# Sixteen row buffers, one block, and one stream of expert rows on VectorE

## The chip, the cores and the metric

The kernel runs on one core of a Trainium2 chip. The metric is the device time of one execution in microseconds, the median of several runs. The work below is done by the core's five engines (TensorE for matrix products, VectorE and ScalarE for elementwise work, GpSimd, which here only issues gathers, and SyncE, which issues the plain DMA transfers) and its 16 DMA engines.

## The reference, cut to what matters

Two networks run one after the other over 256 tokens of width 1024. The first has two layers; each ends in a PEER block. Per token it picks 128 experts of 16384 (8 heads, 16 each), takes a dot product of the token with each expert's row of `peer_u`, and adds up rows of `peer_v` weighted by gate and GELU:

```python
def expert_block(args):
    hb, ib, gb = args
    u = peer_u[ib]
    act = jax.nn.gelu(jnp.einsum('btd,bthkd->bthk', hb, u), approximate=False)
    return jnp.einsum('bthk,bthkd->btd', gb * act, peer_v[ib])
```

The second network has a context branch `z` that doesn't depend on the first network: a feed-forward block, a short convolution, a feed-forward block (its layer 0), then a feed-forward block and the attention's context keys and values (its layer 1):

```python
z = ffn_sublayer(z, mz, 0, g[0], g[1], ffn_w_gu[i, 0], ffn_w_down[i, 0])
hz = adaln_in(z, g[2], mz[3], mz[4])
yz = short_conv_mixer(hz, conv_w_in[j], conv_w[j], conv_w_out[j])
z = adaln_out(z, yz, g[3], mz[5], 1.0)
z = ffn_sublayer(z, mz, 6, g[4], g[5], ffn_w_gu[i, 1], ffn_w_down[i, 1])
```

## The kernel before

The expert phase stands twice in the kernel, once for each layer of the first network. The expert rows are gathered and used beside the context branch of the second network, which needs TensorE and the weights' DMA.

One expert row here means one gather: for each of the 128 tokens of a tile (one per partition) one row of 1024 floats, 512 KB in all. A layer has 512 of them: 256 of `peer_u` (128 for each of two token tiles; called feature rows below) and then 256 of `peer_v` (value rows). `Experts.fetch` (line 1728) issues them from GpSimd, each into the next of `GR = 8` buffers of the arena, after waiting until the row that used the buffer is done (`row_used`). `Experts.use` (line 1763) works on VectorE by heads of 16 rows. A feature row is a multiply and sum with the token's features, which stand in PSUM (line 1792, a custom instruction and a read of its accumulator); its result goes to one of 16 cells, which line 1797 copies out after each head. A value row is a multiply and add into PSUM (line 1788); it waits for its own row (`row_landed`) and for the row before it (`row_used`); line 1777 copies 16 weights into the cells ahead of each head. `enter_tile` (line 1746) changes the token tile.

The context branch is a chain of stages, each a block of its own. At the end of a block all engines meet before any starts the next. In each stage VectorE has the stage's own work and a whole number of heads beside it, written out in the order in which they run:

- `context_norm` (829): ScalarE squares and scales, TensorE turns, ScalarE makes the features. 1 head of rows; the first two rows go ahead of the reciprocal.
- `gate_up` (1886): 11 tiles of 64 matmuls; ScalarE a SiLU (1913) and VectorE a product (1931) for each. 5 heads, 8 rows for each of ten tiles.
- `down` (2040): 8 tiles of 44 matmuls; ScalarE copies and squares. 3 heads.
- `context_add` (2152): a chain of six small and large steps on VectorE (2168 to 2175), then 1 head.
- `conv_projection` (2272): 6 tiles of 64 matmuls; 3 heads. VectorE takes the products of tiles 4 and 5 (2322). `conv_taps` (2329): VectorE alone, 25 instructions, then 1 head. `project_out` (2100): 2 tiles of 32 matmuls, 1 head. `context_keys` (2406): 64 matmuls, 1 head.
- `weigh` (1819): GELU on ScalarE and the product with the gates, both over all 256 cells of a partition. It stands between the feature rows and the value rows.
- `alone` (1802): the heads that are left, in a loop on VectorE, with no context work beside them.

Layer 0 runs ffn z00 (10 heads), conv (6 heads), `weigh`, the convolution's add (1 head), ffn z01 (10 heads), and 5 heads alone. Layer 1 runs ffn z10 (10 heads), norm and keys (2 heads), 4 heads alone, `weigh`, and 16 heads alone.

The weights come through `WeightStream` (line 148): SyncE loads half a tile at a time into `raw`, which holds two tiles. Context weights are used as they are. For other stages they are split into `w_hi` and `w_lo`; these two tensors, 4096 floats each per partition, are idle in the expert phase. The loads of a next stage's first two tiles are issued at the end of the stage before.

TensorE's, ScalarE's and VectorE's programs are written out instruction by instruction in most of these stages; loops stand in `gate_up` (pairs of tiles, on all three) and in `alone` (VectorE). GpSimd's gathers are all written out.

## Time and profile before

| | |
|---|---|
| median of 3 runs | 4243.65 us (4240.59 to 4245.16) |
| the profiled execution's own time | 4238.47 us |
| its span | 4236.7 us |
| expert phase of layer 0 (from its first norm to the last row) | 591.6 to 1567.9 us |
| expert phase of layer 1 | 2131.3 to 2955.5 us |
| busy, of the span: TensorE, VectorE, ScalarE, GpSimd | 64%, 63%, 23%, 23% |

The page cuts the span into 40 slices of about 106 us, a digit for each in tenths. Expert phases are where GpSimd (POOL) is busy:

```profile
PE   6776649937389308676569610000798698977698
DVE  3635686674777795544966778998645555545554
POOL 0000024452454540000044556665000000000000
DMA  6543679997799974432789999998344244541153
```

In the slices of the expert phases DMA stands at 7 to 9 tenths, and the last four of layer 1 have TensorE at 0: these are the rows without context work.

### The profile page before, as it was taken

The page shows a single profiled execution, that of the slowest core. Times are in us where ns is not written, and L with a number is a line of the kernel's source. Part 1 is how long each engine was busy: PE and PEld are TensorE (multiplying, and loading weights), DVE is VectorE, ACT ScalarE, POOL GpSimd, SP SyncE. Part 2 cuts the span into 40 slices and gives each one's busy share as a digit, 9 for nine tenths or more (in the row PEclk, how much of TensorE's full clock was granted, in tenths as well). Part 3 has the DMA queues.
Part 4 walks back from the last instruction along what each step waited for, and adds up shares of the span by engine and source line. Part 5 has one row for each costly group of instructions (what it writes and reads, how often), then busy time and mean ns, then how long its engine had stood idle before and what let it go on. Part 6 is the DMA issues. An engine that isn't in the chain of part 4 may idle for free. (4 is left out here: it accounts for less than half of the span.)

```text
span 4236.7 us, 44741 instructions
## 1 busy us (share of the span) xinstructions
PE 2721.9 (64%) x16804; PEld 2359.7 (56%) x16804; DVE 2673.1 (63%) x3884; ACT 982.5 (23%) x1358; POOL 961.8 (23%) x1028
## 2 busy tenths in 40 slices
PE   6776649937389308676569610000798698977698
PEld 5555428835178307475258610000798598975498
DVE  3635686674777795544966778998645555545554
ACT  2333210010110003332110000000444344533343
POOL 0000024452454540000044556665000000000000
PEclk8978769967699759787679855555899799988899
DMA  6543679997799974432789999998344244541153
GB/s 236 192 160 108 243 310 381 412 374 278 288 390 412 378 296 161 169 128 98 314 310 413 394 347 358 367 377 327 130 158 156 103 160 149 166 144 44 40 186 112
DMA packets 229372, 1034.40 MB, mean 244 GB/s; under 512 B 29657, under 2 KB 32617, under 8 KB 180073
## 3 DMA queue, kind: packets, MB, share of 16 engines
q0 software_dynamic: 147456, 536.94, 32.7%
q1 hardware_dynamic: 81768, 495.51, 32.3%
q8 instruction: 91, 1.49, 0.1%
q14 instruction: 57, 0.46, 0.0%
HBM read 1031.30 MB, written 1.05 MB: 244 GB/s over the span
## 5 line engine op out<-in xcount | busy, mean ns | idle before, releaser
L270 DVE TENSOR_TENSOR w_lo<-raw,w_hi 128x1024 fp32r<-128x1024 f32 (+1 forms) x492 | 558.6, 1138 | 700.2 <-ACT w_hi L257 699.7
L1740 POOL DMA_INDIRECT arena_layer<-in_peer_u,arena_layer x512 | 481.3, 940 | 1632.6 <-SPq L833 1165.8
L1788 DVE SCALAR_TENSOR_TENSOR ps<-arena_layer,ps 128x1024 f32<-128x1024 f32 x512 | 660.2, 1290 | 85.8 <-DMA arena_layer<-in_peer_v,arena_layer 50.8
L1792 DVE CUSTOM_DVE_ANT_0 arena_layer<-arena_layer,ps 128x1024 f32<-128x1024 f32 x512 | 608.8, 1219 | 147.4 <-DMA arena_layer<-in_peer_u,arena_layer 121.5
L628 PE MATMUL ps<-hT_hi,w_hi 128*128 128x256 f32 x2240 | 644.7, 288 | 70.7 <-PEq L763 31.6
L257 ACT ACTIVATE w_hi<-raw 128x1024 fp32r<-128x1024 f32 (+1 forms) x492 | 485.1, 989 | 796.3 <-PE ps L628 795.1
L628 PE MATMUL ps<-hT_lo,w_hi 128*128 128x256 f32 x2240 | 642.8, 287 | 0.0
L628 PE MATMUL ps<-hT_hi,w_lo 128*128 128x256 f32 x2240 | 642.2, 287 | 0.0
L628 PE MATMUL ps<-parts_context,raw 128*128 128x256 f32 x2496 | 568.3, 390 | 94.2 <-issue 78.6
L628 PEld LDWEIGHTS ps<-parts_context,raw 128*128 128x128 f32 x2496 | 487.4, 196 | 174.8 <-issue 106.6
L1740 POOL DMA_INDIRECT arena_layer<-in_peer_v,arena_layer x512 | 480.3, 938 | 351.5 <-DVE ps L1788 251.1
L628 PEld LDWEIGHTS ps<-hT_hi,w_hi 128*128 128x128 f32 x2240 | 437.9, 195 | 74.4 <-issue 74.4
L628 PEld LDWEIGHTS ps<-hT_lo,w_hi 128*128 128x128 f32 x2240 | 437.8, 195 | 0.0
L628 PEld LDWEIGHTS ps<-hT_hi,w_lo 128*128 128x128 f32 x2240 | 437.5, 195 | 0.0
L886 PE MATMUL ps<-ident,adacol 128*128 128x128 f32 x96 | 18.9, 378 | 650.2 <-PEq L1804 627.2
L886 PEld LDWEIGHTS ps<-ident,adacol 128*128 128x128 f32 x96 | 17.7, 284 | 651.1 <-issue 651.1
L628 PE MATMUL ps<-raw,parts_context 128*128 128x256 f32 (+1 forms) x1184 | 277.0, 397 | 24.4 <-issue 24.4
L628 PEld LDWEIGHTS ps<-raw,parts_context 128*128 128x128 f32 x1184 | 228.5, 193 | 71.5 <-issue 41.6
L628 PE MATMUL ps<-w_hi,parts_ffn_x 128*128 128x256 f32 x1408 | 257.8, 286 | 3.7 <-PEq L1891 3.7
L628 PEld LDWEIGHTS ps<-w_hi,parts_ffn_x 128*128 128x128 f32 x1408 | 223.0, 195 | 3.9 <-issue 3.9
L690 PE MATMUL ps<-raw,cond 128*32 128x512 f32 x960 | 171.2, 820 | 80.1 <-DMA raw<-in_w_mod 32.2
L628 PE MATMUL ps<-w_lo,parts_ffn_x 128*128 128x256 f32 x704 | 200.9, 285 | 0.0
(361 smaller groups left out, 2957.4 us busy)
## 6 DMA issues: line engine op xcount, KB each, us to landing
raw<-in_ffn_w_gu SPq DMA_DIRECT2D x154, 1024.0 KB
raw<-in_w_mod SPq DMA_DIRECT2D x72, 1024.0 KB
raw<-in_w_ada SPq DMA_DIRECT2D x48, 1024.0 KB
raw<-in_w_in SPq DMA_DIRECT2D x44, 1024.0 KB
raw<-in_ffn_w_down SPq DMA_DIRECT2D x56, 768.0 KB
raw<-in_ffn_w_down SPq DMA_DIRECT2D x56, 640.0 KB
raw<-in_conv_w_in SPq DMA_DIRECT2D x24, 1024.0 KB
raw<-in_w_o SPq DMA_DIRECT2D x8, 1024.0 KB
```

The lines of the kernel that those rows point to most:

```text
L257: act.activation(self.hi[:, k, 0:g.chunks[k] * g.cols], self.raw_part(g, parity, k // 2, g.starts(k), g.starts(k + 1)), ACT.Copy).then_inc ...
L270: dve.tensor_tensor(self.lo[:, k, 0:n], self.raw_part(g, parity, k // 2, g.starts(k), g.starts(k + 1)), self.hi[:, k, 0:n].bitcast(F32), A ...
L628: mm = pe.matmul(out_, stay, move, start=start and n == 0, stop=stop and n == len(combos) - 1, skip_group_check=True)
L690: mm = pe.matmul(ps[at:at + STRIP, unit, 0:512], cond[:, k, :], part[:, c, :], start=k < STRIPS, stop=k >= KC - STRIPS, skip_group_check=True)
L886: mm = pe.matmul(ps[:, unit, c * P:(c + 1) * P], column(c).to_broadcast([P, P]), ident[:], start=True, stop=True)
L1740: gp.indirect_dma_start(self.grow[:, slot % GR, :], None, self.tables[slot // half_way], bass.IndirectOffsetOnAxis(ap=self.index[:, k:k + ...
L1788: dve.scalar_tensor_tensor(out=self.tile, in0=row, scalar=cell, in1=self.tile, op0=ALU.mult, op1=ALU.add) \
L1792: dve.tensor_tensor_reduce(row, row, self.tile, 1.0, 0.0, ALU.mult, ALU.add, cell).then_inc(row_used.sem, 1)
```

## The change

The whole expert phase of a layer becomes one block. Each engine runs through all stages in its own order. A stage is ordered against the one before it by three new semaphores, one of TensorE, ScalarE and VectorE each; each engine drains and increments its own at the end of its part (`stage_after`, `stage_ended`). VectorE's rows stand partly behind its increment, so that the other engines can go on to the next stage while it works on them.

The gathers are one run of 512 on GpSimd, over 16 buffers; the eight new ones lie over `w_hi` and `w_lo`. VectorE takes rows one by one with `rows(dve, n)`, all written out; heads have no meaning there any more, and neither the 16 cells nor the copies of lines 1797 and 1777 are left: a dot product is written to its place in `acts`, and a value row reads its weight from there. GELU and gates are done for each token tile by itself.

Rows per stage: norm 12 (2 ahead of the reciprocal, 10 behind the increment), gate_up 8 for each of 11 tiles, down 44 (behind the increment), add 2 and 4 behind the increment, conv 32, 8 and 8 (ahead of the products 4 and 5), taps none, convout 16, keys 12. Layer 0 has 382 rows beside context work and 130 behind it; layer 1 has 174 and 338. In `context_keys` the copy of the turned keys moves from VectorE to ScalarE. The functions that the second network's main branch uses lose their context branches and are otherwise the same.

Core of the diff (lines that are only blank in the new code are left out; tensor and scalar programs of the context stages are those of before between `stage_after` and a drain):

```diff
@@ -331,8 +331,10 @@
 
 
     raw = sb("raw", [P, 4, 2 * QUARTER])
+    split_base = nc.sbuf_base
     w_hi = sb("w_hi", [P, QUARTERS, QUARTER], F32R)
     w_lo = sb("w_lo", [P, QUARTERS, QUARTER], F32R)
+    more_rows = nc.alloc_sbuf_tensor_at("expert_rows", [P, 8, D], F32, offset=split_base)
     x_tok = sb("x_tok", [P, TT, D])
     z_tok = sb("z_tok", [P, TT, D])
@@ -419,7 +421,7 @@
     act_ready = signal("act_ready")
     cols_ready = signal("cols_ready")
     halves_landed = [ctx.enter_context(nc.semaphore(f"half_landed_{k}")) for k in range(4)]
-    GR = 8
+    GR = 16
     row_landed = [signal(f"rows_landed_{s}") for s in range(GR)]
     row_used = signal("row_used")
     turned = signal("turned")
@@ -427,8 +429,11 @@
     expd = signal("exponentials_made")
     normalised = signal("normalised")
     summed = signal("summed")
-    dots_kept = signal("dots_kept")
     tile_in_psum = signal("tile_in_psum")
+    gelu_made = signal("gelu_made")
+    context_pe = signal("context_stage_on_pe")
+    context_act = signal("context_stage_on_act")
+    context_dve = signal("context_stage_on_dve")
 
     mod_rows = signal("mod_rows")
...
+    def stage_after(eng, *others):
+
+        for other in others:
+            eng.wait_ge(other.sem, other.base)
+
+    def stage_ended():
+        for signal_ in (context_pe, context_act, context_dve):
+            signal_.base += 1
+
+    def context_norm(block, scale, shift, gain, full, experts, n_rows):
 
 
...
+            act.drain().then_inc(context_act.sem, 1)
+
+        @block.vector
+        def _(dve):
+            stage_after(dve, context_pe, context_act)
+            dve.scalar_tensor_tensor(out=scol[:], in0=scale, scalar=1.0, in1=gain,
+                                     op0=ALU.add, op1=ALU.mult).then_inc(cols_ready.sem, 1)
+            experts.rows(dve, 2)
+            dve.wait_ge(act_ready.sem, act_ready.at(1))
+            dve.reciprocal(stat[:, 4:6], stat[:, 2:4]).then_inc(vec_ready.sem, 1)
+            dve.drain().then_inc(context_dve.sem, 1)
+            experts.rows(dve, n_rows - 2)
+        stage_ended()
         cols_ready.base += 1
...
-    HEADS = 2 * TT * PEER_HEADS
+    ROWS = 2 * TT * SLOTS
...
+            self.next = 0
+        def fetch(self, block):
+            @block.gpsimd
+            def _(gp):
+                for n in range(ROWS):
+                    gp.wait_ge(row_used.sem, row_used.at(n + 1))
+                    k = n % (TT * SLOTS)
+                    gp.indirect_dma_start(
+                        self.grow[n % GR], None, self.tables[n // (TT * SLOTS)],
+                        bass.IndirectOffsetOnAxis(ap=self.index[:, k:k + 1], axis=0)) \
+                      .then_inc(row_landed[n % GR].sem, 16)
+        def activate(self, block, t):
+            @block.scalar
+            def _(act):
+                act.wait_ge(row_used.sem, row_used.at(GR + (t + 1) * SLOTS))
+                part = self.acts[:, t * SLOTS:(t + 1) * SLOTS]
+                act.activation(part, part, ACT.Gelu).then_inc(gelu_made.sem, 1)
+        def enter_features(self, dve, t):
+            dve.wait_ge(row_used.sem, row_used.at(GR + t * SLOTS))
+            dve.tensor_copy(self.tile, self.hf_tok[:, t, :]).then_inc(tile_in_psum.sem, 1)
+            dve.wait_ge(tile_in_psum.sem, tile_in_psum.at(t + 1))
+        def enter_values(self, dve, t):
+            dve.wait_ge(row_used.sem, row_used.at(GR + (TT + t) * SLOTS))
+            if t:
+                dve.tensor_copy(self.y[:, t - 1, :], self.tile).then_inc(tile_in_psum.sem, 1)
+                dve.wait_ge(tile_in_psum.sem, tile_in_psum.at(TT + 2 * t + 1))
+            dve.memset(self.tile, 0.0).then_inc(tile_in_psum.sem, 1)
+            dve.wait_ge(gelu_made.sem, gelu_made.at(t + 1))
+            part = slice(t * SLOTS, (t + 1) * SLOTS)
+            dve.tensor_tensor(self.acts[:, part], self.acts[:, part], self.gate[:, part], ALU.mult) \
+               .then_inc(tile_in_psum.sem, 1)
+            dve.wait_ge(tile_in_psum.sem, tile_in_psum.at(TT + 3 * t + 2))
+        def rows(self, dve, n):
+            for q in range(self.next, self.next + n):
+                values, k = q // (TT * SLOTS), q % (TT * SLOTS)
+                if q % SLOTS == 0:
+                    (self.enter_values if values else self.enter_features)(dve, k // SLOTS)
+                dve.wait_ge(row_landed[q % GR].sem, row_landed[q % GR].at(16 * (q // GR + 1)))
+                row, cell = self.grow[q % GR], self.acts[:, k:k + 1]
+                if values:
+                    dve.wait_ge(row_used.sem, row_used.at(GR + q))
+            self.next += n
+        def rest(self, block, upto):
+            @block.vector
+            def _(dve):
+                self.rows(dve, upto - self.next)
...
+    def context_gate_up(block, name, h, hff, silu, experts, n_rows):
+        weights.begin(f"gu_{name}")
+        n = weights.group().n
+        @block.sync
+        def _(sp):
+            weights.feed(sp)
+        @block.tensor
+        def _(pe):
+            stage_after(pe, context_act, context_dve)
+            def tile(t, j, turn):
+                unit_wait(pe, j, turn)
+                project_features(pe, t, blocks_of(j), (h,), j, turn)
+            in_pairs(n, pe, tile)
+            pe.drain().then_inc(context_pe.sem, 1)
+        @block.scalar
+        def _(act):
+            stage_after(act, context_pe, context_dve)
+            def tile(t, j, turn):
+                product_wait(act, t)
+                unit_wait(act, j, turn)
+                act.activation(silu[:, j, :], ps[:, j, 0:512], ACT.Silu).then_inc(act_ready.sem, 1)
+            in_pairs(n, act, tile)
+            act.drain().then_inc(context_act.sem, 1)
+        @block.vector
+        def _(dve):
+            for t in range(n):
+                experts.rows(dve, n_rows)
+                if t == 0:
+                    stage_after(dve, context_pe, context_act)
+                dve.wait_ge(act_ready.sem, act_ready.at(1 + t))
+                dve.tensor_tensor(hff[:, t * 512:(t + 1) * 512], silu[:, t % 2, :],
+                                  ps[:, t % 2, 512:1024], ALU.mult) \
+                   .then_inc(unit_free[t % 2].sem, 1)
+            dve.drain().then_inc(context_dve.sem, 1)
+        stage_ended()
+        act_ready.base += n
...
+    def context_down(block, name, hff, row, experts, n_rows):
...
+        @block.vector
+        def _(dve):
+            stage_after(dve, context_pe, context_act)
+            gate_columns(dve, *row)
+            dve.drain().then_inc(context_dve.sem, 1)
+            experts.rows(dve, n_rows)
...
+    def context_add(block, parts_y, experts, n_rows):
...
+        @block.vector
+        def _(dve):
+            v = Steps(dve, vec_step)
+            stage_after(dve, context_pe, context_act)
+            sums = stat[:, 32:40].rearrange("p (t g) -> p t g", g=4)[:, :, 0:parts_y]
+            dve.tensor_reduce(stat[:, 0:2], sums, AX_X, ALU.add).then_inc(vec_ready.sem, 1)
+            experts.rows(dve, 2)
+            dve.wait_ge(act_ready.sem, act_ready.at(1))
+            v.link(dve.reciprocal(stat[:, 4:6], stat[:, 2:4]))
+            for t in range(TT):
+                v.link(dve.scalar_tensor_tensor(out=y_tok[:, t, :], in0=y_tok[:, t, :],
+                                                scalar=stat[:, 4 + t:5 + t], in1=ps[:, 3, :],
+                                                op0=ALU.mult, op1=ALU.mult))
+                v.tick(dve.tensor_tensor(z_tok[:, t, :], z_tok[:, t, :], y_tok[:, t, :], ALU.add))
+            dve.drain().then_inc(context_dve.sem, 1)
+            experts.rows(dve, n_rows - 2)
...
+    def context_conv_in(block, h, b_gate, u, up, experts, n_rows):
...
+        @block.vector
+        def _(dve):
+            v = Steps(dve, vec_step)
+            experts.rows(dve, 4 * n_rows)
+            stage_after(dve, context_pe, context_act)
+            v.tick(dve.memset(up[:, :, 0:1], 0.0))
+            v.tick(dve.memset(up[:, :, SEQ + 1:SEQ + 2], 0.0))
+            for t in (4, 5):
+                experts.rows(dve, n_rows)
+                product_wait(dve, t)
+                dve.wait_ge(unit_free[t % 2].sem, unit_free[t % 2].at(3))
+                at = slice(4 * (t - 4), 4 * (t - 3))
+                dve.tensor_tensor(up[:, at, 1:SEQ + 1], u[:, at, :],
+                                  ps[:, t % 2, :].rearrange("p (b t) -> p b t", t=SEQ), ALU.mult) \
+                   .then_inc(unit_free[t % 2].sem, 1)
+            dve.drain().then_inc(context_dve.sem, 1)
...
-        grow = rest[:, 0:GR * D].rearrange("p (r n) -> p r n", r=GR)
-        acts = rest[:, GR * D:GR * D + 256]
+        grow = [rest[:, k * D:(k + 1) * D] for k in range(8)] + [more_rows[:, k, :] for k in range(8)]
+        acts = rest[:, 8 * D:8 * D + 256]
         flat_index = index.rearrange("p t h k -> p (t h k)")
 
 
         begin_parts(f"context_{l}", 2048 + D_FF * TT, F32)
-        experts = Experts(l, hf_tok, flat_index, gate, grow, acts, small)
-        if l == 0:
-            context_ffn("z00", 0, 0, 0, experts, (1, 5, 3, 1))
-            context_conv(experts)
-            context_ffn("z01", 0, 6, 4, experts, (1, 5, 3, 1))
-        else:
-            context_ffn("z10", 1, 0, 0, experts, (1, 5, 3, 1))
-            h, kz = carve((KC, SEQ), (TT, 2 * NKV, HD), of=parts)
-            context_norm_in(1, 3, 2, h, experts, 1)
-            context_keys(h, kz, context_v[:], context_kT[:], experts, 1)
-            experts.alone(HEADS // 2 - experts.done)
-            experts.weigh()
-        experts.alone(HEADS - experts.done)
+        experts = Experts(l, hf_tok, flat_index, gate, grow, acts)
+        with nc.Block(no_gpsimd_drain=True) as block:
+            experts.fetch(block)
+            if l == 0:
+                context_ffn(block, "z00", 0, 0, 0, experts, (12, 8, 44, 6))
+                experts.activate(block, 0)
+                context_conv(block, experts, (12, 8, 16, 6))
+                context_ffn(block, "z01", 0, 6, 4, experts, (12, 8, 44, 6), 1)
+            else:
+                context_ffn(block, "z10", 1, 0, 0, experts, (12, 8, 44, 6))
+                h, kz = carve((KC, SEQ), (TT, 2 * NKV, HD), of=parts)
+                context_norm_in(block, 1, 3, 2, h, experts, 12)
+                context_keys(block, h, kz, context_v[:], context_kT[:], experts, 12)
+                experts.activate(block, 0)
+                experts.activate(block, 1)
+            experts.rest(block, ROWS)
         experts.end()
```

## Rows read from the trace of the kernel before

**Rows 1.** The page's DMA part: queue, packets, MB, share of 16 engines.
```profile
q0 software_dynamic: 147456, 536.94, 32.7%
```

**Rows 2.** Layer 0 by stage: window, us, busy us per engine, PEclk, DMA share, GB/s.
```profile
620.00:783.00 163.00, 157.63 (x704) 137.10 (x704) 103.58 (x176) 12.99 (x16) 76.92 (x82) 0.96 0.98 392
783.00:876.00 93.00, 78.03 (x368) 68.58 (x368) 60.37 (x101) 6.00 (x21) 44.47 (x48) 0.93 1.02 412
876.00:927.00 51.00, 3.67 (x16) 3.27 (x16) 43.00 (x74) 12.14 (x25) 30.68 (x33) 0.50 0.94 363
927.00:1050.00 123.00, 98.29 (x384) 78.10 (x384) 59.56 (x103) 4.05 (x4) 45.11 (x48) 0.81 0.78 291
1050.00:1081.00 31.00, 0.00 (x0) 0.00 (x0) 30.07 (x60) 0.00 (x0) 13.25 (x15) 0.52 0.72 270
1081.00:1124.00 43.00, 34.05 (x80) 16.34 (x80) 19.23 (x34) 4.80 (x11) 16.82 (x18) 0.87 0.90 346
1124.00:1180.00 56.00, 3.68 (x16) 3.28 (x16) 48.28 (x44) 13.65 (x27) 29.11 (x31) 0.52 0.76 279
1180.00:1336.00 156.00, 154.20 (x704) 135.09 (x704) 110.16 (x96) 12.98 (x16) 76.08 (x81) 0.99 1.01 401
1336.00:1429.00 93.00, 79.70 (x368) 69.87 (x368) 64.71 (x55) 5.98 (x20) 44.14 (x47) 0.93 1.02 412
...
1458.00:1568.00 110.00, 0.00 (x0) 0.00 (x0) 104.53 (x86) 0.00 (x0) 69.00 (x74) 0.50 0.95 368
```

**Rows 3.** Layer 1 by stage, the same columns.
```profile
2323.00:2409.00 86.00, 79.70 (x368) 69.90 (x368) 60.20 (x100) 5.97 (x20) 44.14 (x47) 0.97 1.03 408
2409.00:2459.00 50.00, 3.68 (x16) 3.27 (x16) 42.89 (x76) 12.17 (x25) 29.83 (x32) 0.50 0.97 370
2459.00:2482.00 23.00, 16.65 (x72) 14.03 (x72) 3.78 (x10) 0.00 (x0) 1.21 (x2) 0.87 0.78 265
2482.00:2595.00 113.00, 0.00 (x0) 0.00 (x0) 94.94 (x166) 1.70 (x2) 75.16 (x80) 0.50 0.97 371
2595.00:2956.00 361.00, 0.09 (x1) 0.12 (x1) 336.34 (x276) 0.00 (x0) 232.62 (x248) 0.50 0.94 360
```

**Rows 4.** Timeline of VectorE: start us, length us, instruction, count [idle before, releaser].
```profile
1134.80 22.17 DVE L1788 SCALAR_TENSOR_TENSOR ps<-arena_layer,ps 128x1024 f32<-128x1024 f32 x16
...
2482.91 1.22 DVE L1792 CUSTOM_DVE_ANT_0 arena_layer<-arena_layer,ps 128x1024 f32<-128x1024 f32 x1
...
2484.06 1.22 DVE L1792 CUSTOM_DVE_ANT_0 arena_layer<-arena_layer,ps 128x1024 f32<-128x1024 f32 x1
...
2597.74 21.16 DVE L1788 SCALAR_TENSOR_TENSOR ps<-arena_layer,ps 128x1024 f32<-128x1024 f32 x16 [0.21 <-DVE arena_layer L1777]
```

**Rows 5.** Timeline of VectorE: the add's chain, the taps' end, a change of token tile.
```profile
876.01 0.16 DVE L2168 TENSOR_REDUCE stat<-stat 128x2 f32<-128x8 f32 x1 [0.39 <-PEq L2055]
...
881.56 1.23 DVE L2175 TENSOR_TENSOR z_tok<-z_tok,y_tok 128x1024 f32<-128x1024 f32 x1
...
1059.78 2.29 DVE L2353 TENSOR_TENSOR parts_context<-rows,parts_context 128x2048 f32<-128x2048 f32 x1
...
2776.06 1.22 DVE L1756 COPY arena_layer<-ps 128x1024 f32<-128x1024 f32 x1
```

**Rows 6.** Timeline of TensorE in gate_up, and inside its stretch in conv.
```profile
977.69 0.59 PE L628 MATMUL ps<-parts_context,raw 128*128 128x256 f32 x1 [2.21 <-issue]
...
1180.57 154.20 PE L628 MATMUL ps<-parts_context,raw 128*128 128x256 f32 x704 [15.24 <-ACTq L833]
```

**Rows 7.** Timeline of ScalarE in the norm ahead of conv.
```profile
904.56 2.19 ACT L857 ACTIVATE y_tok<-z_tok,stat 128x1024 f32<-128x1024 f32 x2 [0.23 <-issue]
...
907.83 2.91 ACT L863 ACTIVATE parts_context<-ps,modcol,scol 128x128 f32<-128x128 f32 x8 [1.08 <-issue]
...
923.64 2.90 ACT L863 ACTIVATE parts_context<-ps,modcol,scol 128x128 f32<-128x128 f32 x8 [12.90 <-remote]
```

**Rows 8.** Timeline of GpSimd while no buffer is missing.
```profile
2430.31 0.94 POOL L1740 DMA_INDIRECT arena_layer<-in_peer_u,arena_layer  x1 [0.30 <-issue]
```

571 lines of the change are left out of this document (263 added, 308 removed).

## The prediction, on record before the run

> **What bounds the kernel now.** I read the page first, then the windows by stage, then the timelines of single engines. No engine is busy for more than 64% of the span, so an average over the span says nothing; the stages do. The change touches the two expert phases only (976 us in layer 0, 825 us in layer 1); everything else I leave at its time.
>
> The first thing to see is the price of a gather on the DMA side. 1024 gathers moved 536.94 MB [rows 1], 0.524 MB each. The DMA engines at their limit show a share of 1.02 and 412 GB/s, as in layer 0's down stages [rows 2]. So a row costs 524/412 = 1.273 us of DMA. GpSimd can issue one in 0.94 + 0.30 = 1.24 us [rows 8], just below; it bounds nothing by itself.
>
> The second is VectorE's price. Feature rows follow each other at 2484.06 - 2482.91 = 1.15 us [rows 4]: cheaper than the DMA's 1.273. Value rows stand in two forms. Written out, 16 take 22.17 us, so the distance is (22.17 - 1.29)/15 = 1.392 us; in the loop it is (21.16 - 1.29)/15 = 1.325 us, and with the copy of 16 weights ahead of each head (the next run of 16 starts 21.69 us after the last one) 1.356 us per row [rows 4]. Value rows without context work are therefore VectorE's, not the DMA's.
>
> The third is where DMA is not at its limit: 363 GB/s in add and norm, 291 in conv, 270 in taps and the head behind them, 279 in the second add and norm [rows 2]; in layer 1 370, 265, 371 [rows 3]. With 8 buffers a head's worth of other work on VectorE empties the gather queue, and in add and norm TensorE stands idle (3.7 of 51 and of 56 us busy) because every block waits for VectorE's 16 rows. Inside gate_up and down, DMA is at 401 to 412 GB/s with TensorE busy for 154 of 156 us: little is left there.
>
> **The change part by part.** Weights by stage, from rate times time less the gathers that GpSimd issued: gate_up 0.401 x 156 = 62.6 MB less 81 x 0.524 gives 20.1 MB or 49 us of DMA; down 0.412 x 93 = 38.3 less 48 x 0.524 gives 13.1 MB or 32 us [rows 2].
>
> *First norm, gate_up, down (both layers).* The block ended with 14 rows behind the reciprocal, 14 x 1.15 to 1.273 = 16 to 18 us. Now TensorE starts when ScalarE is done: from L857's start to the end of the first eight L863 are 6.2 us, and eight more take 2.9, so 9.1 us [rows 7]. Gain 8 us. gate_up then has 88 rows: 88 x 1.273 + 49 = 161 us of DMA against 154 of TensorE [rows 6]; before it took 163 with 80. Down has 44 rows: 56 + 32 = 88 us against 93. Row count at its end is 144 in both kernels. Gain 8 + 2 + 5 = 15 us: layer 0's down ends at 861 and not 876, layer 1's at 2394 and not 2409. (Layer 1's down took 86 [rows 3]; the bound from the other side is 12 us.)
>
> *Add and norm before conv.* The add's chain takes 882.8 - 876.0 = 6.8 us [rows 5], and two rows of 1.15: 9 us. VectorE increments its semaphore there, and four rows plus the norm's two (6.9 us) run beside ScalarE's squares; then the 9.1 us of above. With a little for drains 26 us instead of 51. TensorE starts conv at 887, not 927. Nothing hid this work before; what hides it from the DMA now are the 16 buffers (20 us of DMA).
>
> *Conv.* 384 matmuls at 154.20/704 = 0.219 us are 84 us [rows 6], but the stage took 123. TensorE executed them one at a time with pauses up to 2.21 us that the profile calls issue [rows 6], while the gathers ran at full rate. ScalarE has a pause of the same look, 12.90 us ahead of L863 [rows 7]. I read both as an engine that waits for its own instructions behind gathers. The code of TensorE in this stage isn't changed, and gathers will again run at full rate, so I take 123 us again; the ends are 84 and, if doubled, 162. It ends at 1010.
> The Trainium skill (Runtime: NRT & Kernel Launch, section Instruction fetch mechanics) says the sequencer fetches the next block of instructions by a DMA queue of its own while it executes the current one, and that the crossing is mostly hidden. By it conv would take 84 us and the phase end 39 us sooner; the row of 2.21 us speaks against it here.
>
> *Taps, output projection, add and norm.* From 1050 to 1062.1 the taps take 12 us [rows 2, 5]; the output projection 43 [rows 2]. Sum: 1022, 1065. Before, 16 rows stood between the two (1050 to 1081) and TensorE waited. Add and norm again 26 to 27 instead of 56, since value rows come only at row 256: 1092 against 1180.
>
> *z01.* 88 rows and the weights are 161 us of DMA; VectorE's share per tile, 8 x 1.392 + 0.7 = 11.8 us, lies under it. 1253. Down 88: 1341, against 1429. Up to here 88 us are gained, but with 376 rows done against 416: 40 rows fewer.
>
> *The rows left alone.* Add 9 us, then 4 + 130 rows. They are written out: 134 x 1.392 = 187 us, plus 3 us for a token tile (the copy is 1.22 [rows 5]; the clearing and the gates' product with their waits are an estimate from it). End 1540, against 1568. So of the 88 us, 60 are given back: 40 rows more at the end, and 0.036 us more for each. Layer 0: **28 us**. The loop of the old kernel was the faster form by 0.067 us a row; what is saved is its copy. Dropping 64 small copies a layer is in these per-row prices.
>
> *Layer 1.* From 2394: add and norm 26, keys 23 as before [rows 3]: 2443, with 174 rows used and, at 1.273 each, about 182 landed (190 is the most). 82 feature rows remain: 82 x 1.15 = 94 us on VectorE, (256 - 184) x 1.273 = 92 on DMA. 2537, against 2595, where GELU's table load and a block stood too; GELU of the first tile is now long done, that of the second lies beside value rows. 256 value rows x 1.392 = 356, two token tiles 6: 2899. The old window of 361 us holds 16 x 21.69 = 347, so some 14 us of it are changes of tile and pauses [rows 3, 4]; I leave 8 of pauses in: 2907, against 2956. Layer 1: **49 us**.
>
> *Costs at nothing.* Drains and three semaphores per stage lie where block ends stood; the move of the keys' copy to ScalarE is off the path; the longer program of VectorE is taken to be fetched in time (even at 0.7 us an instruction, an estimate from the 2.21 us pauses as three of these, a row's two instructions take 1.4 us, 0.13 more than the DMA's price). Nothing is queued behind GpSimd's waits but gathers. SyncE's loads pass no new wait.
>
> **Sum.** 28 + 49 = 77 us. The execution's own time of 4238.5 becomes 4161.5; on the median of 4243.65 the forecast is 4167.
>
> **Rivals.**
> *Better: TensorE isn't starved in conv.* It starts with fewer rows behind it and other code blocks. The 39 us then go, 116 in all: 4128. For it: down, also written out, ran 352 matmuls with no pause in 93 us windows. Against it: the same code in the same company.
>
> *Slower: instructions wait behind 16 gathers.* The 12.90 us pause is about ten gathers of 1.273. If a fetch waits for what is in flight, 16 buffers double it. Price: conv's 39 us twice (+39), the same 39 in each of three down stages, which are written out too (+117), and 13 us more in each of three norms (+39): 195 us against a gain of 77, 4362. It decides from 77 us of such pauses on. For it: both pauses fall where gathers run back to back. Against it: DMA was full in down too, and nothing paused.
> The Trainium skill (DMA: Bandwidth & Descriptors, section Queues, rings and completion order) says each DMA engine takes turns between the queues that have work. By that a fetch would not wait for a whole queue of gathers, and a deeper queue would cost it nothing; no row here shows it either way, and the sum above doesn't use it.
>
> *No change: weights wait behind the gathers.* If at the start of each of eight weight stages 16 rows and not 8 go ahead of the weights, TensorE waits 8 x 1.273 = 10 us each time, 82 in all: 4249. Against it: VectorE's rows are tied to tiles, so the gathers run out of buffers and the weights catch up.
>
> **Chances.** Forecast 0.64 (its own range 4130 to 4215), better 0.17, slower 0.14, no change 0.05. A difference under 0.2% (8 us) is no change for this kernel's measurement. Faster 0.81, within 0.05, slower 0.14. The range is 4105 to 4250: the low end is the better case with value rows at 1.325 ((134 + 256) x 0.067 = 26 us more), the high end the case of no change.
>
> **What would show it.** In the windows after: DMA at 400 GB/s or more through add, norm and conv; conv's matmuls starting near 887; 51 and 56 us between down and conv, and between projection and gate_up, shrunk to about 27; 16 value rows at the end at 22.2 us; last row of layer 0 near 1540 and layer 1's phase near 776 us long. Wrong: pauses of 1 us or more between TensorE's matmuls in down, ScalarE pauses of 20 us, or value rows at 1.325. The forecast falls if TensorE's windows in gate_up grow beyond 165 us.

## The result and the profile after

The changed kernel is slower, by 1.3%. Its median is 4303.09 us (4291.35 to 4316.62, 4 runs) beside 4244.4 us (4240.59 to 4275.11, 4 runs) for the kernel before; the ratio is 1.0131, with an interval of 1.0097 to 1.0165. The forecast was 4167 us, and 4250 was the high end of its range. The profiled execution took 4291.35 us, with a span of 4289.6 us against 4236.7. The ratios in this document are formed from undisturbed runs (one run of the kernel before that took 8721.47 us on chip D, below, is among those left out), and aren't always the quotient of the medians beside them.

First the page after, with the lines that answer to the four slices shown of before:

```profile
PE   6776749677698008676569730000698697977698
DVE  3625676744677985444956478999655554545554
POOL 0000034523454630000054356665000000000000
DMA  6543689977899964433689889998344244541153
```

The expert phases still look full, so the stages have to be read. The windows answer to [rows 2] (first fence) and [rows 3] (second fence), with the same columns.

```profile
611.00:793.00 182.00, 159.30 (x704) 136.52 (x703) 112.00 (x193) 12.99 (x16) 95.64 (x102) 0.93 0.99 394
793.00:916.00 123.00, 90.09 (x368) 72.03 (x368) 52.84 (x91) 5.41 (x18) 41.33 (x44) 0.81 0.85 327
916.00:941.00 25.00, 3.99 (x17) 3.62 (x18) 23.85 (x41) 15.51 (x32) 13.31 (x15) 0.63 0.76 267
941.00:1066.00 125.00, 97.66 (x384) 78.12 (x383) 60.31 (x104) 4.05 (x4) 48.72 (x52) 0.81 0.82 311
...
1078.00:1113.00 35.00, 31.89 (x80) 15.84 (x80) 18.78 (x35) 4.82 (x11) 15.05 (x16) 0.93 0.90 345
1113.00:1137.00 24.00, 3.81 (x17) 3.45 (x18) 23.54 (x40) 10.66 (x24) 13.39 (x15) 0.52 0.72 258
1137.00:1302.00 165.00, 156.85 (x704) 136.10 (x704) 121.34 (x117) 13.80 (x17) 86.88 (x92) 0.97 0.99 395
1302.00:1386.00 84.00, 81.60 (x368) 71.05 (x368) 56.85 (x45) 6.60 (x22) 41.32 (x44) 0.96 1.02 412
...
1405.00:1585.00 180.00, 0.14 (x1) 0.17 (x2) 165.43 (x130) 0.00 (x0) 105.20 (x112) 0.50 0.91 351
```

```profile
2354.00:2477.00 123.00, 90.16 (x368) 71.92 (x368) 51.92 (x91) 5.97 (x20) 41.36 (x44) 0.82 0.80 306
...
2501.00:2536.00 35.00, 22.34 (x72) 16.83 (x72) 19.91 (x40) 0.41 (x1) 15.04 (x16) 0.73 0.99 393
2536.00:2647.00 111.00, 0.00 (x0) 0.00 (x0) 94.65 (x162) 2.32 (x4) 76.11 (x81) 0.51 0.98 378
2647.00:3008.00 361.00, 0.00 (x0) 0.00 (x0) 333.09 (x261) 0.18 (x1) 227.35 (x241) 0.50 0.93 354
```

The second row is the surprise: the down stage has the same 368 matmuls, but 123 us where it had 93 with its head of rows, and the clock is 0.81 and not 0.93. The same stands in layer 1's first row. The third down stage (1302:1386) has nothing of it. TensorE's timeline inside the first down stage shows what happened (start, length, instruction, count, idle before it):

```profile
795.77 15.06 PE L632 MATMUL ps<-raw,parts_context 128*128 128x256 f32 x69
...
823.75 0.58 PE L632 MATMUL ps<-raw,parts_context 128*128 128x256 f32 x1 [2.21 <-issue]
826.56 0.58 PE L632 MATMUL ps<-raw,parts_context 128*128 128x256 f32 x1 [2.22 <-issue]
...
857.55 57.46 PE L632 MATMUL ps<-raw,parts_context 128*128 128x256 f32 x257 [0.83 <-issue]
```

It is the pause of [rows 6], in a stage that had none: TensorE goes from 69 matmuls at full speed to one matmul every 1.4 to 2.8 us from 811 to 857.5, waiting for nothing that the profile shows, and then runs 257 without a gap. These distances are near multiples of 0.7 us (2.81 is 4 x 0.70). GpSimd, over the border of the pause:

```profile
853.32 0.58 PE L632 MATMUL ps<-raw,parts_context 128*128 128x256 f32 x1 [0.84 <-issue]
```
```profile
852.68 0.94 POOL L1750 DMA_INDIRECT expert_rows<-in_peer_u,arena_layer  x1 [0.30 <-issue]
854.27 0.94 POOL L1750 DMA_INDIRECT expert_rows<-in_peer_u,arena_layer  x1 [0.65 <-remote]
918.27 0.94 POOL L1750 DMA_INDIRECT arena_layer<-in_peer_u,arena_layer  x1 [63.06 <-DVE arena_layer L1802]
```

The last gather that found a free buffer went out at 854.27; 3.3 us later TensorE was at full speed again. Then no gather was issued for 63 us: VectorE had done the stage's 44 rows, all 16 buffers were full, and TensorE still had 257 of its 352 products before it. Layer 1's down stage shows the same border: the last gather of the run went out at 2414.94, TensorE is at full speed from 2418.21, again 3.3 us later, and the next gather is issued at 2478.55.

```profile
2416.82 0.79 PE L632 MATMUL ps<-raw,parts_context 128*128 128x256 f32 x1 [0.64 <-issue]
2418.21 6.14 PE L632 MATMUL ps<-raw,parts_context 128*128 128x256 f32 x21 [0.61 <-issue]
```
```profile
2414.94 0.94 POOL L1750 DMA_INDIRECT expert_rows<-in_peer_u,arena_layer  x1 [0.50 <-remote]
2478.55 0.94 POOL L1750 DMA_INDIRECT arena_layer<-in_peer_u,arena_layer  x1 [62.67 <-DVE arena_layer L1802]
```

The windows of the first one, split at the border:

```profile
811.00:857.00 46.00, 15.72 (x26) 7.34 (x27) 35.22 (x61) 0.00 (x0) 29.43 (x32) 0.53 1.03 410
857.00:916.00 59.00, 57.46 (x257) 49.88 (x256) 0.00 (x0) 5.41 (x18) 0.00 (x0) 0.96 0.66 237
```

In the first TensorE stands at the lower of its two clock levels (0.53) with DMA at its limit; in the second its clock is back at 0.96, VectorE and GpSimd do nothing, and DMA falls to 0.66. Each engine is idle while the other could have worked. By TensorE's products alone (start of the first to end of the last), down took 119.2 and 118.9 us instead of 76.1 and 77.4; gate_up 180.5 and 184.4 instead of 161.2 and 161.6; conv 124.1 (121.5), z01's gate_up 162.7 (154.2), z01's down 78.7 (77.4), the keys 30.9 (15.5), the output projection 28.3 (36.4). Two of the signs that the prediction had named for being wrong are there: pauses between the products in down, and gate_up beyond 165 us.

### The profile page after: what moved, and what is told of

It reads as the page before. It is cut to its first block and busy times, and to the rows that moved or that the text cites. A ratio compares the mean times of both kernels' runs of the same rounds, so it can differ in the third digit from the quotient of the medians.

```text
span 4289.6 us, 44125 instructions
## 1 busy us (share of the span) xinstructions
PE 2762.3 (64%) x16804; PEld 2370.5 (55%) x16804; DVE 2643.4 (62%) x3820; ACT 985.1 (23%) x1362; POOL 964.1 (22%) x1028
## 5 line engine op out<-in xcount | busy, mean ns | idle before, releaser
L632 PEld LDWEIGHTS ps<-parts_context,raw 128*128 128x128 f32 x2496 | 489.9, 197 | 179.6 <-issue 112.1
L1750 POOL DMA_INDIRECT arena_layer<-in_peer_u,arena_layer x256 | 240.7, 940 | 1533.5 <-POOLq L1633 1179.0
L632 PE MATMUL ps<-raw,parts_context 128*128 128x256 f32 (+1 forms) x1184 | 304.3, 412 | 76.2 <-issue 75.4
L1798 DVE SCALAR_TENSOR_TENSOR ps<-arena_layer,ps 128x1024 f32<-128x1024 f32 x256 | 329.7, 1288 | 37.6 <-DMA arena_layer<-in_peer_v,arena_layer 11.7
L1798 DVE SCALAR_TENSOR_TENSOR ps<-expert_rows,arena_layer,ps 128x1024 f32<-128x1024 f32 x256 | 329.7, 1288 | 34.8 <-DMA expert_rows<-in_peer_v,arena_layer 6.3
L1802 DVE CUSTOM_DVE_ANT_0 arena_layer<-arena_layer,ps 128x1024 f32<-128x1024 f32 x256 | 299.2, 1217 | 24.1 <-DMA arena_layer<-in_peer_u,arena_layer 11.9
L1802 DVE CUSTOM_DVE_ANT_0 expert_rows<-expert_rows,ps 128x1024 f32<-128x1024 f32 x256 | 298.7, 1217 | 11.9 <-issue 10.8
L1750 POOL DMA_INDIRECT expert_rows<-in_peer_u,arena_layer x256 | 240.6, 940 | 182.8 <-DVE arena_layer L1802 112.0
L1750 POOL DMA_INDIRECT expert_rows<-in_peer_v,arena_layer x256 | 242.1, 946 | 166.8 <-DVE ps L1798 95.6
L1750 POOL DMA_INDIRECT arena_layer<-in_peer_v,arena_layer x256 | 240.5, 939 | 139.0 <-DVE ps L1798 77.4
```

The costliest lines, as they stand in the source:

```text
L632: mm = pe.matmul(out_, stay, move, start=start and n == 0, stop=stop and n == len(combos) - 1, skip_group_check=True)
L1750: gp.indirect_dma_start(self.grow[n % GR], None, self.tables[n // (TT * SLOTS)], bass.IndirectOffsetOnAxis(ap=self.index[:, k:k + 1], axis ...
L1798: dve.scalar_tensor_tensor(out=self.tile, in0=row, scalar=cell, in1=self.tile, op0=ALU.mult, op1=ALU.add) \
L1802: dve.tensor_tensor_reduce(row, row, self.tile, 1.0, 0.0, ALU.mult, ALU.add, cell).then_inc(row_used.sem, 1)
```

## Experiments

Theories, as they stood when the experiments began and as they grew. **Buffers:** more gathers in flight make an engine's instructions late. **Block:** not the buffers but the one block and its order do it. **In flight, not buffers:** the 16 places are harmless, 16 transfers under way are not. **Self-feeding:** a pause lasts as long as gathers run back to back; VectorE's rows of a stage are tied to nothing, so they keep the gathers running while TensorE stands, and the remedy is to tie rows to TensorE's tiles. **Order of waits:** the written-out value row costs 1.392 us because it waits first for its data and then for the row before. In the expectations Buffers is Theory A (A' where only some chips have it), Block is Theory B and Self-feeding Theory D; Theory C is that 8 buffers starve VectorE at the stage changes, and Theory E that a pause has its own length.

The runs fell on four chips, which matters more than expected. I call them A, B, C, D. B and D have the pauses and run the kernel before in about 4245 us, like the run of the result, whose chip isn't on record; A and C have none and run it in about 4156 us. B was used twice, at two times, and was the same both times; A, C and D were used once, so that what belongs to the chip and what to the time of the run isn't told apart. Every time of a stage below comes from one profiled execution of its version.

**Chip A: one part at a time.** The changed kernel with 8 buffers:

```diff
-    GR = 16
+    GR = 8
-        grow = [rest[:, k * D:(k + 1) * D] for k in range(8)] + [more_rows[:, k, :] for k in range(8)]
+        grow = [rest[:, k * D:(k + 1) * D] for k in range(8)]
```

> The new kernel with 8 row buffers instead of 16 and nothing else changed. Theory A (TensorE's pauses in down, conv and gate_up come from gathers in flight; 16 buffers let twice as many queue): the pauses in the two down stages (40 us each in the new kernel) go, down takes 90 to 95 us, and the time is 4200 to 4245. Theory B (the one block and VectorE's written-out rows do it, by their own instruction stream): the pauses stay, 4290 or more. Theory C (8 buffers also starve VectorE at the stage changes): pauses gone, but add and norm lose what they gained, 4240 to 4260.

The opposite edit, the kernel before with those 16 places (`GR = 16` and the same list):

> The kernel before with 16 row buffers (the 8 new ones where the changed kernel has them) and nothing else changed. Theory A: down in z00 and z10 gets pauses of about 40 us each as in the changed kernel; the time is 4260 to 4300. Theory B: no new pauses; the deeper buffers fill the holes at stage changes, 4215 to 4244.

The changed kernel with 16 buffers but fewer gathers under way; 8, and the same with 4 in place of both 8s:

```diff
                     gp.wait_ge(row_used.sem, row_used.at(n + 1))
+                    if n >= 8:
+                        m = n - 8
+                        gp.wait_ge(row_landed[m % GR].sem, row_landed[m % GR].at(16 * (m // GR + 1)))
```

> The changed kernel with its 16 buffers, but a gather is issued only when the one 8 before it has landed, so at most 8 are in flight. Theory A in the form in flight: like 8 buffers for the pauses, 16 for the holes: 4180 to 4235. If it is the run of gathers at full rate and not their number in flight: pauses stay, 4280 to 4310.

> The same with at most 4 gathers in flight (4 x 1.273 = 5.1 us of queue). Theory A: pauses short or none in conv too, DMA still at 400 GB/s or more beside weights; 4150 to 4200. Full-rate theory: conv and down keep their pauses of about 40 us, 4280 to 4310.

Measured against 4156.89 us: new with 8 buffers 4141.33 (0.9966, 0.9953 to 0.9978), old with 16 buffers 4122.54 (0.9916, 0.9899 to 0.9932), new with 8 in flight 4125.8 (0.9925, 0.9908 to 0.9942), new with 4 in flight 4314.85 (1.0379, 1.0358 to 1.0401). None had the pauses of the trace after (down took 76.1 to 76.9 us and conv 84.5 to 86.0 in all four), and the kernel before was 87 us faster than in its first runs; so this chip couldn't tell the theories apart. The expectations had all been set for the slower chip and were missed: three runs came out below every range, and the fourth, with 4 in flight, above both of its ranges. It showed two things: 16 buffers by themselves are worth 34 us in the old order when nothing pauses, and 4 gathers are too few to feed the rows. The windows of the last kernel, gate_up and the rows alone:

```profile
611.00:784.00 173.00, 160.35 (x704) 138.05 (x704) 109.16 (x180) 12.71 (x16) 79.80 (x86) 0.96 0.98 380
1336.00:1572.00 236.00, 0.23 (x2) 0.00 (x0) 190.88 (x152) 3.07 (x7) 130.17 (x139) 0.51 0.90 320
```

320 GB/s where the version with 8 in flight has 347 in its rows alone, and 380 against 413 in gate_up. The likely reason is that one gather's way there and back is no longer covered by the others; that wasn't tried by itself.

**Chip B: the same again, with both kernels unaltered beside them.**

> The changed kernel unaltered, beside the kernel before on the same chip. On the chip of the first four runs the kernel before took 4157 us, 87 less than where the forecast was measured, and none of those runs had TensorE's pauses. Theory A' (instructions are fetched late only in some placements, chips or processes; there, more gathers in flight make it worse): where the kernel before takes about 4157, this takes 4085 to 4125 and has no pauses; where the kernel before takes about 4244, this takes 4290 to 4320 with its pauses. Theory B (16 buffers and one block together always bring the pauses): 4230 or more even where the kernel before takes 4157.

> The kernel before unaltered, for its trace on the same chip. Where its time is about 4157: conv's 384 matmuls in 85 us instead of 121.5, value rows at the same 1.392 and 1.325, layer 0's last row near 1515 instead of 1568. Where it is about 4244: the pauses of the first trace again.

> The changed kernel with 8 buffers again, on whatever chip this is. Where the kernel before takes 4244 and the changed one 4300: Theory A says the pauses in down go and the time is 4200 to 4245; Theory B says 4290 or more. Where the kernel before takes 4157: 4141 as in the first run, about 25 more than the changed kernel.

> The kernel before with 16 buffers again. Where the kernel before takes 4244: Theory A says new pauses in down and 4260 to 4300. Where it takes 4157: 4123 as in the first run, without pauses.

Against 4246.81: new 4286.91 (1.01, 1.0061 to 1.0139), new with 8 buffers 4228.2 (0.9953, 0.9928 to 0.9978), old with 16 buffers 4355.78 (1.0263, 1.0229 to 1.0297); the kernel before alone gave 4238.33, with the pauses of its first trace. Theory A's ranges held for 8 buffers (4200 to 4245); the other two lie outside, 4286.91 just below 4290 to 4320, and 4355.78 far above 4260 to 4300, because in the old order gate_up (173.5 and 181.1 us) and z01's down (93.5) paused as well. The three changed ones in layer 0's first down stage, and the last two in conv; one fence each, new, new with 8, old with 16:

```profile
789.00:908.00 119.00, 88.19 (x360) 71.05 (x359) 52.45 (x89) 4.48 (x15) 41.34 (x44) 0.81 0.88 337
```
```profile
791.00:867.00 76.00, 76.00 (x353) 66.74 (x351) 49.18 (x80) 4.48 (x15) 37.12 (x41) 1.00 1.02 412
900.00:1032.00 132.00, 99.39 (x384) 78.65 (x384) 60.03 (x102) 4.32 (x5) 47.26 (x51) 0.79 0.78 288
```
```profile
798.00:917.00 119.00, 88.73 (x357) 71.29 (x355) 55.27 (x98) 4.48 (x15) 45.03 (x48) 0.81 0.84 319
970.00:1092.00 122.00, 95.41 (x384) 77.34 (x384) 57.18 (x102) 4.05 (x4) 45.14 (x48) 0.82 0.78 292
```

This down stage is 119 us with 16 buffers in either kernel and 76 with 8: that settles Buffers against Block, for this stage. Layer 1's is less clean: 119.6 and 119.2 us with 16, but 101.7 in the new order with 8, where the kernel before had 77.4; so 8 lessen the pause and don't exclude it. In conv the number of buffers makes no difference: its products take 130.0 us with 16 and 131.0 with 8 in the new order, 121.4 with 16 and 122.2 with 8 in the old. A two by two of medians: in the old order 16 buffers cost 4355.78 - 4246.81 = 109 us, in the new one 4286.91 - 4228.2 = 59. The rest of the change is worth 19 us with 8 buffers and 69 with 16.

**Chip C: tying, and the order of waits.** Rows tied to TensorE's tiles, in down and in conv:

```diff
@@ context_down, VectorE
-            experts.rows(dve, n_rows)
+            for g in range(4):
+                experts.rows(dve, n_rows // 4)
+                if g < 3:
+                    product_wait(dve, 2 * g + 1)
@@ context_conv_in, VectorE
-            experts.rows(dve, 4 * n_rows)
-            stage_after(dve, context_pe, context_act)
+            for t in range(4):
+                experts.rows(dve, n_rows)
+                if t == 0:
+                    stage_after(dve, context_pe, context_act)
+                product_wait(dve, t)
```

> The changed kernel, with VectorE's rows in down and conv tied to TensorE's tiles: 11 rows, then a wait for the product of a pair of tiles, in down; 8 rows, then a wait for the product of a tile, in conv. So gathers stop, 16 rows later, when TensorE stops. Theory D (a pause feeds itself: while TensorE waits for instructions it uses no weights, the gathers take the whole DMA rate and hold it off until the rows of the stage run out): on a chip with pauses (kernel before about 4247), the pauses of about 45 us in down and conv shrink to 25 or less and the time is 4190 to 4250 against 4287. Theory E (a pause has its own length, whatever the gathers do): pauses as before, 4280 to 4320. On a chip without pauses: within 10 us of the changed kernel.

> The changed kernel with at most 8 of its 16 buffers in flight, again. On a chip with pauses: if what counts is the number in flight, pauses as with 8 buffers and 4215 to 4240; if what counts is that VectorE frees buffers quickly and gathers run back to back, 4280 to 4300 as with 16. On a chip without: 4126 as in the first run.

A value row's two waits in the other order, first for the row before, then for its data:

```diff
-                dve.wait_ge(row_landed[q % GR].sem, row_landed[q % GR].at(16 * (q // GR + 1)))
                 row, cell = self.grow[q % GR], self.acts[:, k:k + 1]
                 if values:
                     dve.wait_ge(row_used.sem, row_used.at(GR + q))
+                dve.wait_ge(row_landed[q % GR].sem, row_landed[q % GR].at(16 * (q // GR + 1)))
+                if values:
```

> The changed kernel with the two waits of a value row in the other order: first for the row before it, then for its own gather. If the 1.392 us of a written-out value row against the loop's 1.325 come from the order in which the waits reach VectorE, rows come to 1.325 and 256 + 134 of them save 0.067 us each, 26 us. If they come from having two waits at all, nothing changes (within 5 us).

> The changed kernel unaltered beside the others. On a chip with pauses 4280 to 4305 as twice before. On a chip without (kernel before about 4157) 4085 to 4125: the forecast's better rival, whose gain was 116 us, with the kernel before starting from 87 us less.

Against 4154.9: new unaltered 4128.58 (0.9932, 0.9916 to 0.9949), tied 4127.26 (0.9932, same interval), 8 in flight 4125.93 (0.9928, 0.9912 to 0.9945), waits swapped 4100.1 (0.9869, 0.9853 to 0.9886). Tying does nothing where nothing pauses, as it must. The swap is worth 28 us (26 expected). The unaltered kernel, expected at 4085 to 4125, is just above. VectorE's timeline with the swap, which answers to [rows 4]:

```profile
1311.55 10.56 DVE L1798 SCALAR_TENSOR_TENSOR ps<-arena_layer,ps 128x1024 f32<-128x1024 f32 x8
1322.15 10.56 DVE L1798 SCALAR_TENSOR_TENSOR ps<-expert_rows,arena_layer,ps 128x1024 f32<-128x1024 f32 x8
```

Eight rows start 10.60 us apart from the next eight, 1.325 us each; without the swap, in the trace after, it is 11.14:

```profile
1405.64 11.04 DVE L1798 SCALAR_TENSOR_TENSOR ps<-arena_layer,ps 128x1024 f32<-128x1024 f32 x8
1416.78 11.03 DVE L1798 SCALAR_TENSOR_TENSOR ps<-expert_rows,arena_layer,ps 128x1024 f32<-128x1024 f32 x8
```

So in written-out code the order of the waits is what 0.067 us a row hang on, as the theory had it. Why the old kernel's loop has 1.325 isn't explained by it: its source (`Experts.use`, line 1763) waits for the data first and for the row before last, like the written-out rows at 1.392. The unaltered changed kernel on this chip, in gate_up, down, add and norm, conv, and the rows alone:

```profile
609.00:769.00 160.00, 156.65 (x704) 136.58 (x704) 109.79 (x182) 12.63 (x16) 89.37 (x96) 0.97 1.02 413
783.00:860.00 77.00, 77.00 (x356) 67.61 (x354) 50.65 (x84) 4.48 (x15) 38.60 (x42) 0.99 1.02 412
860.00:888.00 28.00, 3.73 (x18) 3.27 (x16) 24.19 (x41) 16.11 (x33) 14.33 (x16) 0.62 1.02 410
888.00:974.00 86.00, 85.60 (x384) 74.85 (x384) 58.60 (x99) 4.37 (x5) 46.30 (x50) 0.97 1.02 413
1313.00:1493.00 180.00, 0.19 (x1) 0.22 (x2) 165.38 (x130) 0.00 (x0) 105.14 (x112) 0.50 0.90 346
```

This is the schedule that the change was drawn for: DMA at 410 to 413 GB/s from the first gate_up to the end of conv (411 in the 14 us between gate_up and down, too).

**Chip B again: the remedies where it hurts.**

> The kernel before unaltered, for its trace on this chip. On a chip without pauses (about 4156): conv's 384 matmuls in 85 us and not 121.5, the output projection in 28, rows alone in layer 1 without the gaps of the first trace; down and gate_up as before. On a chip with pauses: the first trace again.

> The changed kernel with 16 buffers and at most 8 in flight. On a chip with pauses: 4215 to 4240 if the number in flight counts, 4280 to 4300 if the freeing of buffers by VectorE does. On a chip without: 4126.

> The changed kernel with both: rows in down and conv tied to TensorE's tiles, and the waits of a value row swapped. On a chip without pauses: 4099, the swap's 28 us and nothing from the tie. On a chip with pauses: Theory D (a pause feeds itself) 4165 to 4220, with pauses of 25 us or less in down and conv; Theory E (own length) 4255 to 4290.

> The changed kernel with 8 buffers and the waits of a value row swapped. On a chip without pauses: 4141 - 28 = 4113. On a chip with pauses: 4228 - 26 = 4202, the better of the two kernels there if the tie doesn't help.

Against 4246.16: 8 in flight 4215.49 (0.9905, 0.9871 to 0.9938), tied and swapped 4152.64 (0.9749, 0.9701 to 0.9797), 8 buffers and swapped 4216.17 (0.9949, 0.9914 to 0.9983); the kernel before alone 4234.81, with the pauses. The swap on top of 8 buffers was to save 26 us and saved 12 (4228.2 to 4216.17): there z01's down, with value rows, took 83.0 us where it had been 76.1. Down and conv with 8 in flight, and then tied and swapped, with add and norm between:

```profile
789.00:866.00 77.00, 76.41 (x356) 66.97 (x355) 49.65 (x81) 5.03 (x16) 35.70 (x39) 1.00 1.02 412
912.00:1030.00 118.00, 96.43 (x384) 77.44 (x384) 48.41 (x83) 4.62 (x6) 42.63 (x46) 0.83 0.81 303
```
```profile
801.00:878.00 77.00, 76.19 (x352) 66.33 (x350) 48.42 (x85) 5.16 (x17) 39.66 (x43) 1.00 1.02 412
878.00:908.00 30.00, 3.64 (x16) 3.27 (x16) 28.60 (x49) 15.76 (x32) 16.92 (x18) 0.63 1.02 411
908.00:999.00 91.00, 87.77 (x384) 75.64 (x384) 53.79 (x95) 4.15 (x5) 45.13 (x48) 0.95 1.01 401
```

With 16 places and 8 under way, down is at 76 us in layer 0 and 77.2 in layer 1: it is the transfers in flight, not the memory that they go to. But conv stays paused at 117. In gate_up it is the places that count more: 179.6 us with 16 in flight, 175.1 with 16 places and 8 in flight, 164.8 with 8 buffers. The pause at its start ends 5 to 7 us after the first long run of gathers in each (638.4 after 632.7, 641.6 after 635.1, 630.1 after 625.2), and the run is longer where there are more places to fill.

In the tied and swapped version, with 16 under way, down goes from 118.2 us to 76.6 and conv from 130.0 to 90.5 (the unaltered one on this chip first), and the rows left for add and norm keep DMA at 411 where the unaltered had 256. It is the tie that does this: the swap touches value rows only, and these two stages have feature rows. The tie alone was never run on a chip with pauses, so its share of the 134 us isn't measured. 4152.64 is also below the range of the theory, 4165 to 4220, since the pauses in down are gone and not only shortened. VectorE's timeline shows the tie at work: in the middle of down it waits for TensorE, and GpSimd issues nothing between 811.44 and 821.39:

```profile
819.89 1.22 DVE L1802 CUSTOM_DVE_ANT_0 expert_rows<-expert_rows,ps 128x1024 f32<-128x1024 f32 x1 [9.73 <-PE ps L632]
```

Pauses remain at the start of gate_up in both layers (the stages take 182.5 and 180.9 us), where 18 rows, ten of the norm and eight of the first tile, run before VectorE first waits for a tile.

**Chip D: does it hold elsewhere, and is 8 in flight worth anything beside the tie?**

> Rows tied and waits swapped, again. On a chip without pauses (kernel before about 4156): 4099, as with swapped waits alone. On the chip with pauses: 4153 again, with down in 76 us and conv in about 90.

> The same with at most 8 gathers in flight. On a chip with pauses: gate_up in 175 us or less instead of 181 in z00 and z10, and 4135 to 4150. On a chip without: 4099, no difference.

Against 4244.89: tied and swapped 4152.1 (0.9785, 0.9708 to 0.9862), the same with 8 in flight 4152.67 (0.9791, 0.9714 to 0.9869). The first gate_up is shorter with 8 in flight (175.1 against 185.0 us), down and conv are alike (76 and 77, 90 and 89), and in the whole it comes to nothing where 4135 to 4150 was expected. The kernel before ran from 4217.69 to 4280.11 us here, and both intervals reach past 0.98, so that the gain here may be under 2%. Tied and swapped is the fastest version on chips with pauses: by the medians 93 us below the kernel before on both, and on chip B 134 us below the changed kernel. It wasn't run on a chip without pauses.

## Why the prediction was wrong

**The steps that held.** TensorE starts the phase 9.6 us sooner (8 forecast). Add and norm take 25.7 us (26), the second 26.7 (27). Conv took 124 (123), which is partly luck: it is 130 us in the same kernel on chip B and 86 on chip C. Written-out value rows cost 1.392 us; layer 0's last stretch, from the end of z01's down, took 199.9 us (199). On chip C nearly the whole working stands: down ends at 860.3 (861 forecast), conv starts at 888.4 (887); with conv at 86 us, the better rival, the last row of layer 0 comes at 1492.4, where the forecast less 39 gives 1501. The median of 4128.58 there is the better rival's 4128, with errors that cancel: taps and output projection take 49 us for 55, z01's gate_up and down 234 for 249, the feature rows alone in layer 1 116 for 94. The kernel before is 87 us faster on such a chip too, so the gain there is 26 us and not 77. No trace of it without pauses exists; the nearest is the old order with 16 buffers on chip A, where conv takes 84.5 us (121.5 before) and gate_up 154.6 (161.2).

**The step that failed** is a default, not a sum. The working read conv's 39 us as instructions waiting behind gathers and then took them as conv's own, put pauses in gate_up, down and keys at nothing, and didn't ask what 16 gathers in flight would do to them: "The code of TensorE in this stage isn't changed, and gathers will again run at full rate, so I take 123 us again". Gate_up and down were priced by DMA and TensorE alone, 161 and 88 us. By its terms, against the measured (start to start):

| term | forecast, us | measured, us |
|---|---|---|
| gate_up z00, z10 | 161, 161 | 180.5, 184.4 |
| down z00, z10, with the gap ahead | 88, 88 | 123.8, 124.4 |
| keys | 23 | 30.9 |
| feature rows alone in layer 1 | 94 | 110.6 |
| taps and output projection | 55 | 45.3 |
| everything else, both layers | | in sum as forecast |

(Keys run from TensorE's first product to its last, the rows alone from there to the last feature row.) That is 19.5 + 23.4 + 35.8 + 36.4 + 7.9 + 16.6 - 9.7 = 130 us, and the profiled execution is 4291.35 - 4161.5 = 130 us over its sum. Of these, 115 are TensorE's pauses by place (gate_up and down); that they vanish together in the trace of chip C (159.7 and 76.8 us) supports it. The 16.6 us are another error, and pauses have no part in it, for on chip C the same rows take 116.2 us. VectorE was to be the limit at 1.15 us a row. It was for the first 40 of the 82 rows, from 2534.5 to 2580.3; the other 42 took 61 us from 2581.4 on, with DMA busy to 0.97 or more and moving 363 to 380 GB/s. The price of 1.273 us was read where DMA moves 412; in the rows alone it is 378 here [the second fence above] and was 371 before [rows 3]. Smaller slips of the working change little: (256 - 184) x 1.273 stands where about 182 rows had landed, 4128 - 26 is 4102 and not 4105, and "DMA is at 401 to 412 GB/s" leaves out the first gate_up's 392.

**Of what hides the DMA's work** "the 16 buffers (20 us of DMA)" were to serve add and norm at 400 GB/s or more. Measured were 267 and 258: ahead of the first of them the buffers were full long before the stage began, as the 63.06 us of GpSimd show. Sixteen buffers are a cover for VectorE's absence only where they are empty when it comes.

**The rival.** "Slower: instructions wait behind 16 gathers" had the mechanism, and its price was out in detail: 39 us in each of three down stages were 43 and 41.5 in two and 1.3 in the third; conv, to be doubled, didn't change; the norms got no pause; and gate_up, not in its list, lengthened by 19 and 23. Its main argument against, "DMA was full in down too, and nothing paused", was the misreading: down was full with 8 in flight. A stage without pauses at one depth says nothing of the stage at twice that depth. And a smaller sign in the trace before was passed over: the first gate_up of each layer took 161.2 and 161.6 us where z01's took 154.2, and three of its products, from 631.9 to 636.8, stand 1.4 to 2.1 us apart like those of conv. The third down stage differs by what its rows cost: value rows at 1.392 us are slower than the DMA's 1.273, so gathers wait for VectorE and don't run back to back; feature rows at 1.15 let them. That this is why it is spared wasn't tried by itself, and it isn't the whole of it: in the old order with 16 buffers that stage took 93.5 us.

**What would hide a late instruction.** By the Trainium skill (Runtime: NRT & Kernel Launch, section Instruction fetch mechanics) the crossing to the next block of instructions is mostly hidden. On chips A and C no run speaks against that; on B and D it would be in the open for up to 46 us at a time, if late instructions are what the pauses are. By the Trainium skill (DMA: Bandwidth & Descriptors, section Queues, rings and completion order) each DMA engine takes turns between the queues that have work. The prediction concluded from this that a deeper queue of gathers costs a fetch nothing; on the same condition, the 119 and 76 us of chip B speak against that conclusion.

**What is shown and what is inferred.** Shown: the pause in layer 0's down comes with 16 gathers in flight and not with 8 (119 against 76 us in both orders; 76 with 16 places and 8 in flight); with 16 it ends 2 to 4 us behind the last gather of the run in the down stages with feature rows, one in each layer, of three traces (after, and both orders on chip B); tying rows ends the pauses in down and most of them in conv; they occur on some chips only. The end of the gathers isn't a rule for all: conv's pause in the trace after ended at 992.6, and gathers went on to 1002.4. Inferred: that TensorE lacks instructions. For it speak the steps of 0.7 us with no releaser. Against a simple form of it, the packets of the instruction queue that the traces record took about 1.0 us each, with pauses and without. What differs between the chips, why conv pauses with 8 in flight while layer 0's down doesn't, and why layer 1's down takes 101.7 us with 8 buffers but 77.2 with 16 buffers and 8 in flight, stays open.

## What to carry to other kernels

In this kernel, side work that feeds on DMA at its limit had to be tied to the progress of the engine that it runs beside; free-running, it finished early, held that engine up while it lasted (119 against 77 us in down), and left DMA at 237 to 267 GB/s behind it. A pause without a releaser that sits where transfers run back to back may belong to the transfers and not to the stage: price it in every stage where the change brings such transfers. And a difference of 2% between chips can change a verdict's sign (the same change was 1.0% slower on chip B and 0.7% faster on chip C), so a change of depth should be timed on more than one.

## What the runs showed of the hardware that was not expected

- The kernel before takes about 4156 or about 4245 us depending on the chip; the changed one 4129, or 4287 to 4303. On the slower chips TensorE has pauses, the longest of 46 us, in which it runs one matmul in 1.4 to 2.8 us.
- The order of two waits ahead of a written-out VectorE instruction: first the wait for the data, mostly met by then, and then the wait for the row before costs 1.392 us a row; the other way round 1.325.
- Gathers of 512 KB need more than four in flight: gate_up ran at 380 GB/s and the rows alone at 320 with four, at 413 and 347 with eight, at 413 and 346 with sixteen (chips A and C). Between eight and sixteen these rates don't differ, only what TensorE suffers on chips B and D.
